# A transformer feed-forward reordered: up-projection bank by bank, half a down-projection per column tile, weight low parts on the vector engine

## What is computed

```python
def conv_gated_mlp(h, w_up, conv_w, conv_b, w_down):
    u = h @ w_up
    up = jnp.pad(u, ((0, 0), (1, 1), (0, 0)))
    u = up[:, :-2] * conv_w[0] + up[:, 1:-1] * conv_w[1] + up[:, 2:] * conv_w[2] + conv_b
    g, val = u[..., :D_FF], u[..., D_FF:]
    return (jax.nn.silu(g) * val) @ w_down
...
        x = x + jnp.concatenate([o_a, o_b, o_c], axis=-1) @ w_out[l]
        h = rmsnorm(x, norm_ffn[l])
        x = x + conv_gated_mlp(h, w_up[l], conv_w[l], conv_b[l], w_down[l])
```

## Time and profile before

| what | value |
|---|---|
| device time, median of 3 runs | 3556.5 us (3555.27 to 3556.6) |
| span of the profiled execution, first to last instruction | 3553.3 us |
| median time less that span | 3.2 us |
| mean granted TensorE clock | 0.943 of full speed |
| PE busy, share of the span | 88% |
| DVE / ACT / POOL busy | 61% / 39% / 31% |
| mean DMA traffic | 56 GB/s |

### The profile page before, as it was taken

How to read it: one execution, slowest core, us unless ns; L and a number is a source line. 1 busy time by engine, 2 the same in 40 slices (tenths; PEclk the granted TensorE clock), 3 DMA queues, 4 the chain that set the end, 5 groups by cost and what they waited for, 6 DMA issues and landing times.

```text
span 3553.3 us, 40957 instructions
## 1 busy us (share of the span) xinstructions
PE 3109.8 (88%) x13488; PEld 2397.5 (67%) x13488; DVE 2156.1 (61%) x2515; ACT 1396.9 (39%) x1917; POOL 1116.9 (31%) x532
## 2 busy tenths in 40 slices
PE   6888999667999999999799889986689999999996
PEld 5666777344777777777666667754467777777775
DVE  5864877997264445444567378779943545444545
ACT  3215888665321222111222188876633221111213
POOL 3113555552332112211221155455424112211222
PEclk8999999878999999999899999997889999999997
DMA  4332111111111111111033321111021111111112
GB/s 152 83 95 80 48 48 47 47 30 72 48 48 47 35 35 59 47 35 47 24 104 83 99 70 54 37 57 39 15 89 42 48 35 59 47 35 35 52 43 59
DMA packets 233542, 198.27 MB, mean 56 GB/s; under 512 B 49344, under 2 KB 207808, under 8 KB 233408
## 3 DMA queue, kind: packets, MB, share of 16 engines
q1 hardware_dynamic: 233408, 196.66, 18.2%
HBM read 163.07 MB, written 33.55 MB: 55 GB/s over the span
## 4 chain that ended last, share of the span: by engine, by line
PE 61%; DVE 17%; issue 14%; ACT 4%; DMA 2%; POOL 1%; DVEq 1%; ACTq 0%; SPq 0%; POOLq 0%
PE ps L1321 37%; PE ps L1533 10%; PE ps L1419 4%; PE ps L1450 4%; DVE ps L1137 2%; DVE ptl L1179 2%; PE ps L1430 2%; PE ps L1431 2%; DVE r L1080 1%; DVE xT L1249 1%; ACT prob L851 1%; DVE cv L1224 1%; PE ps L1462 1%; DVE rinv L1154 1%; ACT pth L881 1%
## 5 line engine op out<-in xcount | busy, mean ns | idle before, releaser
L1321 PE MATMUL ps<-xgh,w0h 128*128 128x512 f32 x1472 | 482.4, 409 | 65.3 <-DVE xT L1249 15.7
L1321 PE MATMUL ps<-xgh,w0l 128*128 128x512 f32 x1472 | 469.5, 400 | 0.0
L1321 PE MATMUL ps<-xgl,w0h 128*128 128x512 f32 x1472 | 468.6, 400 | 0.0
L1218 DVE TENSOR_TENSOR u<-ps,rstd 128x512 f32<-128x512 f32 x176 | 109.2, 683 | 581.3 <-PE ps L1321 581.0
L1450 PE MATMUL ps<-cst,prob 128*128 128x128 f32 x2048 | 334.9, 289 | 121.1 <-DVE prob L1155 58.0
L1450 PEld LDWEIGHTS ps<-cst,prob 128*128 128x128 f32 x2048 | 256.1, 147 | 270.1 <-DVE ptl L1179 140.9
L1419 PE MATMUL ps<-stack 128*128 128x512 f32 (+1 forms) x1152 | 349.0, 425 | 100.3 <-ACT prob L851 81.8
L1179 DVE TENSOR_TENSOR ptl<-ps,pth 128x512 fp32r<-128x512 f32 x512 | 348.7, 686 | 142.2 <-ACT pth L881 136.2
L851 ACT ACTIVATE prob<-ps,nmx 128x1024 f32<-128x1024 f32 x320 | 356.7, 1115 | 83.1 <-DVE nmx L1141 61.5
L955 ACT ACTIVATE cv<-u,vec 128x1024 f32<-128x1024 f32 x88 | 104.7, 1238 | 723.6 <-DVE u L1218 723.6
L1321 PEld LDWEIGHTS ps<-xgh,w0h 128*128 128x128 f32 x1472 | 279.8, 193 | 155.2 <-issue 28.0
(11 more groups left out here) (168 smaller groups left out, 5206.4 us busy)
## 6 DMA issues: line engine op xcount, KB each, us to landing
wraw<-in_w_up SPq DMA_DIRECT2D x88, 512.0 KB, 4.2
draw<-in_w_down SPq DMA_DIRECT2D x22, 1024.0 KB, 7.5
wraw<-in_w_in SPq DMA_DIRECT2D x36, 512.0 KB, 4.1
x_d<-xT SPq DMA_DIRECT2D x2, 4096.0 KB, 15.4
raw<-qa_d SPq DMA_DIRECT2D x32, 256.0 KB, 3.7
raw<-ka_d SPq DMA_DIRECT2D x32, 256.0 KB, 4.0
vraw<-v_d SPq DMA_DIRECT2D x32, 256.0 KB, 2.9
wraw<-in_w_out SPq DMA_DIRECT2D x16, 512.0 KB, 4.9
```

What stands on the lines that cost most here:

```text
L1218: ins = dve.tensor_tensor(u[:, c, 1 + b * HALF:1 + (b + 1) * HALF], ps[:, 4 * par + 2 * c + b, :], rstd[:, b * HALF:(b + 1) * HALF], ALU.mult)
L1321: ins = pe.matmul(outs[b], a, x_[:, b * HALF:(b + 1) * HALF], start=start and n == 0, stop=stop and n == 2)
```

## The change

The feed-forward is rewritten in steps of one column tile on every engine.

- PE: `up(f)` goes bank by bank: for each `c` and each token half `b` all 24 matmuls of that bank in a row, and `up_done` is raised after each bank. Tiles from 2 on always use banks 0 to 3; tile 1 uses 4 to 7. After each `up(f)` from `f` = 2 on comes one half (8 of 16 outputs) of the `down` of the group before, in banks 4 to 7. The first half's outputs too now wait for adds of four outputs before.
- DVE: `conv_in` is per `c`; the eight adds of the half `down` stand between `conv_in(f, 1)` and `outer_taps(f, 1)`. DVE also makes the low parts of the weights (`lo_up` of tiles 2 to 21, `lo_down` of groups 1 to 10); POOL keeps those of tiles 0 and 1 and group 0.
- ACT: `mid_tap` is per `c`, with the SiLU between the two; one `hi_up` in each step and one `hi_down` in each second step.
- `ah` and `al` have four slots for two; the loop runs four tiles long (`run_steps`: 4 tiles ahead of the loop, 4 passes of 4, 2 behind it). The program is built with `dynamic_dma_scratch_size=1024`, and SP's code is as it was.

```diff
-STEPS = {"pool layer": 24, "pool units": 2, "dve layer": 246, "dve units": 0, "dve group": 6}
+STEPS = {"pool layer": 24, "pool units": 2, "dve layer": 246, "dve units": 0, "dve quad": 12}
+QUAD = 4
+QUADS = 4
-        ah, al = sb(ph3, "ah", [P, 2, T], F32R), sb(ph3, "al", [P, 2, T], F32R)
+        ah, al = sb(ph3, "ah", [P, QUAD, T], F32R), sb(ph3, "al", [P, QUAD, T], F32R)
+        def run_steps(fn, eng, step=None):
+
+            for q in range(QUAD):
+                fn(0, q)
+            with eng.Fori(1, 1 + QUADS) as m:
...
+                for q in range(QUAD):
+                    fn(m, q)
...
+            for q in range(FT - QUAD * (1 + QUADS)):
+                fn(1 + QUADS, q)
```

POOL and ACT:

```diff
                 lo_up(1, 1)
                 lo_down(0)
-                lo_up(2, 0)
-                with pool.Fori(1, GROUPS - 1) as i:
-                    lo_up(i * 2 + 1, 1)
-                    lo_up(i * 2 + 2, 0)
-                    lo_down(i)
-                lo_up(FT - 1, 1)
-                lo_down(GROUPS - 1)
...
+                def act_step(m, q):
+
+                    f = m * QUAD + q
+                    mid_tap(f, 0)
+                    gate(f)
+                    mid_tap(f, 1)
+                    if not (isinstance(f, int) and f >= FT - 2):
+                        hi_up(f + 2, q % 2)
+                    hi_a(m, q)
+                    if q % 2 and not (isinstance(f, int) and f == 1):
+                        hi_down(m * 2 + q // 2)
```

DVE:

```diff
+                def lo_up(f, par):
+
+                    dve.wait_ge(up_hi, l * (KT + FT) + KT + f + 1)
+                    dve.tensor_tensor(up_weights(par)[1][:, :], wraw[:, :], up_weights(par)[0][:, :].bitcast(F32), ALU.subtract).then_inc(up_lo, 1)
...
+                def dve_ffn(m, q):
+
+                    f = m * QUAD + q
+                    first = isinstance(f, int)
+                    conv_in(f, 0)
                     outer_taps(f, 0)
+                    conv_in(f, 1)
+                    if not (first and f < 2):
+                        for j in range(8):
+                            add_down(m * 2 + (q // 2 - 1), 8 * (q % 2) + j)
                     outer_taps(f, 1)
+                    if not (first and f >= FT - 2):
+                        lo_up(f + 2, q % 2)
                     gate_value(f)
-                    lo_a(f, f)
...
+                    lo_a(f, q)
+                    if q % 2 and not (first and f == 1):
+                        lo_down(m * 2 + q // 2)
```

PE:

```diff
-                    for k in range(KT):
-                        if first and f == 0:
-                            pe.wait_ge(xg_lo, l * 16 + 8 + k + 1)
-                        for c in range(2):
-                            o = (2 * k + c) * P
-                            outs = [ps[:, 4 * par + 2 * c + b, :] for b in range(2)]
-                            ins = three(outs, up_weights(par)[0][:, o:o + P], up_weights(par)[1][:, o:o + P], xgh[:, k, :], xgl[:, k, :], k == 0, k == KT - 1)
-                    ins.then_inc(up_done, 1)
...
+                    base = 4 if first and f == 1 else 0
+                    for c in range(2):
+                        if not (first and f == 1):
+                            pe.wait_ge(u_ready, l * (2 * FT) + f * 2 - 1 + c)
+                        for b in range(2):
+                            for k in range(KT):
+                                o = (2 * k + c) * P
+                                for n, (a, x_) in enumerate(((wh, xgh), (wl, xgh), (wh, xgl))):
+                                    ins = pe.matmul(ps[:, base + 2 * c + b, :], a[:, o:o + P], x_[:, k, b * HALF:(b + 1) * HALF],
+                                                    start=k == 0 and n == 0, stop=k == KT - 1 and n == 2)
+                            ins.then_inc(up_done, 1)
...
-                        if j >= 4:
+                        if j >= 4 or not (isinstance(g, int) and g == 0):
                             pe.wait_ge(y_done, l * (16 * GROUPS) + g * 16 + j - 3)
...
+                def pe_step(m, q):
+
+                    f = m * QUAD + q
+                    up(f, q % 2)
...
+                    elif not (isinstance(f, int) and f == 1):
+                        pe.wait_ge(u_ready, l * (2 * FT) + f * 2)
+                        down(m * 2 + (q // 2 - 1), 2 - q // 2 * 2, 8 * (q % 2), 8 * (q % 2) + 8)
+
+                run_steps(pe_step, pe)
+                down(GROUPS - 1, (2 * GROUPS - 2) % QUAD, 0, 16)
```

More of the change, by code:

```diff
@@ L962, in gate, with hi_a @@
                     act.activation(cv[:, 0, :], cv[:, 0, :], ACT.Silu).then_inc(silu_done, 1)
[L964 to L974, removed]
-                gate(1)
-                hi_a(1, 1)
-                def act_group(i, last):
-                    mid_taps(i * 2)
-                    hi_up(i * 2 + 1, 1)
-                    gate(i * 2)
-                    if not last:
-                        hi_up(i * 2 + 2, 0)
-                    hi_a(i * 2, 0)
-                    hi_down(i)
-                    mid_taps(i * 2 + 1)
-                    gate(i * 2 + 1)
-                    hi_a(i * 2 + 1, 1)
-                with act.Fori(1, GROUPS - 1) as i:
-                    act_group(i, False)
-                act_group(GROUPS - 1, True)
-                act.wait_ge(up_done, l * FT + FT)
+                def hi_a(m, q):
+                    act.wait_ge(prod_done, l * FT + m * QUAD + q + 1)
+                    if not (isinstance(m, int) and m == 0):
+                        act.wait_ge(down_done, l * (16 * GROUPS) + m * 32 + (q // 2 * 16 - 16))
+                    act.activation(ah[:, q, :], cv[:, 0, :], ACT.Copy).then_inc(a_hi, 1)
+                def act_step(m, q):
[8 more added lines that the diff above has]
+                        hi_down(m * 2 + q // 2)
+                run_steps(act_step, act)
+                act.wait_ge(up_done, l * (4 * FT) + 4 * FT)
                 for n in range(2):
@@ L1523, in down @@
-                def down(g):
+                        for k in range(KT):
+                            pe.wait_ge(xg_lo, l * 16 + 8 + k + 1)
+                            for c in range(2):
+                                o = (2 * k + c) * P
+                                for n, (a, x_) in enumerate(((wh, xgh), (wl, xgh), (wh, xgl))):
+                                    for b in range(2):
+                                        ins = pe.matmul(ps[:, 2 * c + b, :], a[:, o:o + P], x_[:, k, b * HALF:(b + 1) * HALF],
+                                                        start=k == 0 and n == 0, stop=k == KT - 1 and n == 2)
+                                        if k == KT - 1 and n == 2:
+                                            ins.then_inc(up_done, 1)
@@ new lines, in up @@
+                        return
+                    if first and f == 1:
+                        pe.wait_ge(root_done, l + 1)
+                    base = 4 if first and f == 1 else 0
+                    for c in range(2):
+                        if not (first and f == 1):
+                            pe.wait_ge(u_ready, l * (2 * FT) + f * 2 - 1 + c)
+                        for b in range(2):
+                            for k in range(KT):
+                                o = (2 * k + c) * P
+                                for n, (a, x_) in enumerate(((wh, xgh), (wl, xgh), (wh, xgl))):
+                                    ins = pe.matmul(ps[:, base + 2 * c + b, :], a[:, o:o + P], x_[:, k, b * HALF:(b + 1) * HALF],
+                                                    start=k == 0 and n == 0, stop=k == KT - 1 and n == 2)
+                            ins.then_inc(up_done, 1)
```

96 lines of the change are left out of this document (33 added, 63 removed).

## The result

| | before | after |
|---|---|---|
| device time, median | 3555.9 us (3549.2 to 3556.6, 4 runs) | 3433.1 us (3429.9 to 3436.3, 4 runs) |
| span of the profiled execution | 3553.3 us | 3428.0 us |
| mean granted clock | 0.943 | 0.954 |

The ratio is 0.9653, 95% interval 0.9636 to 0.9671. The forecast was 3411 us with a range of 3402 to 3444. The time is inside the range, but it is that of rival 1 (3435 us), not of the likeliest case.

What follows compares the result with a forecast made beforehand. PE was taken to set the pace, with 117.5 us of surplus in the feed-forwards. Terms 117.5 + 14.0 - 10.0 + 23.8 = 145.3 us off 3553.3 give 3408.0; the median's 3.2 more makes 3411 us, range 3402 to 3444.

Steps and rivals of the forecast that it cites:

- rival 1: In `up`: the pace stays at 0.2324 us a matmul, 23.8 us of gain are missing, 3435 us; chance 0.34.
- the likeliest case: Whole kernel: all four terms hold, `up` taking `down`'s pace, 145.3 us gained, 3411 us; chance 0.46.
- stalls inside the groups: Feed-forward loop: PE runs through without waiting for DVE, regaining all 117.5 us of surplus in two layers.
- end of a layer: Ahead of the last `down`: PE's wait falls from 14.23 to 7.2 us, 14.0 gained in all.
- start of a layer: At `up(2)`: a new 3.4 us wait for `u_ready`, 5.0 a layer with slow matmuls, 10.0 lost in all.
- pace of `up`: In `up`: matmul spacing falls from 0.2324 to `down`'s 0.2265 us, 23.8 us gained over 4032 matmuls.
- Rival 3: On DVE: taps take 5.37 us without POOL too, PE waits 5.3 us a step, 3689 us; chance 0.04.
- I take the row that the new form is nearest to: In `up`: `down`-like form, new weights each matmul and 24 in a row per bank, was taken to give 0.2265 us.
- Rival 2: In the steps: PE's clock drops, 1.65 us in each of 40, 3477 us; chance 0.12 with other small waits.
- Rival 4: In the longer loop: instructions arrive late at branches, eating the gain, 3556 us; chance 0.04 with anything leaving time unchanged.
- The low end of the range: At the start of a layer: no wait of PE at `up(2)`, given as 3402 us.

Runs made afterwards that it cites:

- e1: Changed kernel with the low parts of the weights made on POOL again (also written e1_pool_lows); 3446.8 us, ratio 0.9701.
- e3: Kernel before with only the weights' low parts moved to DVE, from tile 3 and group 1 on, taps still between the adds; 3466.9 us, ratio 0.9763.
- e2b_pairs_half: Changed kernel with `up` in halves by `c`, matmul pairs sharing a weight block and alternating between two banks; 3432.1 us, ratio 0.9662.
- p1_incs: Changed kernel with one more semaphore increment at every sixth matmul of `up`, which nothing waits on; 3433.1 us, ratio 0.9648.
- p4_down_weights_up: Changed kernel with `down` of groups 0 to 9 taking its weights from `up`'s buffers, so its output is not the feed-forward's; 3434.4 us, one run.
- p3_down_reads_x: Changed kernel with `down` of groups 0 to 9 reading `xgh`, `xgl` as moving operand, so its output is not the feed-forward's; 3442.7 us, one run.
- p5_align: Changed kernel with the constants allocated ahead of `xgh` and `xgl`, which then start at multiples of 1024 bytes; 3410.3 us, ratio 0.9578.
- p6_shift_ah: Changed kernel with 128 bytes of padding ahead of `ah` and `al`, so they start 128 past a multiple of 1024; 3441.0 us, ratio 0.9667.
- i1_ends: Changed kernel with `up(2)` waiting only for tile 0 and the last `down`'s weights split ahead of `hi_a` and `lo_a`; 3426.7 us, ratio 0.9632.
- b2_before_align: Kernel before with the constants allocated ahead of `xgh` and `xgl`, which then start at multiples of 1024 bytes; 3517.4 us, ratio 0.9882.

## Why the prediction was right, and where it was wrong

By its own terms, per layer, from the start of `up(1)` to the start of the last `down`:

| term | predicted, us | measured, us |
|---|---|---|
| stalls inside the groups | -58.7 | -58.7: nothing of the surplus is left, PE busy 643.28 of 643.28 |
| end of a layer | -7.0 | -4.2: 10.06 for 14.23 |
| start of a layer | +5.0 | +1.9: 1017.06 - 992.75 = 24.31 for 1017.08 - 994.67 = 22.41 |
| pace of `up` | -11.9 | +1.8: 0.2333 for 0.2324, 2016 matmuls |
| sum | -72.6 | -59.2 worked out; -59.1 and -59.3 measured |

- **Stalls: right.** DVE was in time in every step, and the tap, the subtraction and the add cost what the rows before had shown. Rival 3 falls: the taps are short once POOL's subtraction isn't beside them (e1, e3). But the change has two remedies for one stall, and with only one of them most of it is gone.
- **Pace of `up`: wrong, and as large as the whole miss.** It is 13.7 us a layer, 27 in all, and the time came out 22 above the forecast. The step that failed is "I take the row that the new form is nearest to". Form had nothing to do with it: e2b_pairs_half has the old form and the new form's pace, p1_incs and p4_down_weights_up leave it, p3_down_reads_x, p5_align and p6_shift_ah move it by the moving operand alone. Rival 1 had the right reason, operands and buffers that don't change, with 0.34. The argument against it, that the paces are steady within each form, was true just as much for "within each operand", and the rows couldn't tell the two apart. The 0.2333 for 0.2324 is a second, smaller thing: p6_shift_ah has 0.2324 in the same order, and p3_down_reads_x has 0.2333 in its first layer and 0.2324 in its second, so it isn't the order either; what makes it stays open.
- **End of a layer: right in kind, 2.8 us short.** The sum followed only the path through `al`. It missed that `hi_down` and `lo_down` of group 10 are queued behind `hi_a` and `lo_a`, though both are in the diff. i1_ends took 2.0 us of it back.
- **Start of a layer: wait there, over-priced by 3.1 us.** `up(2)` came 1.9 us later (1.65 of idle time) and not 3.4. Of the 1.5 between, 1.3 is the SiLU's table load, which ACT made at 1002.01 us (`1002.01 1.28 ACT L970 ACT_TABLE_LOAD`), while the taps were still running on DVE, instead of in the serial path. The 1.65 us for slow matmuls didn't come: none followed this wait. They did in p5_align, and in one layer of two in e1_pool_lows; what decides it is open, and the rows of before couldn't price it.
- **Rival 2 didn't come**: granted clock 1.00 over 643 us, with a bank handed over every 5.6 us. The Trainium skill's warning on bank cycling (TensorE: Matmul & The Clock Gate, A second HAM failure mode: psum-queue depth-cycling) isn't borne out by this row. **Rival 4 didn't come** either: the steps are all 33.28 us, those with a branch among them.
- **What was luck.** The time lies in the range because the range took in rival 1; with the likeliest case alone it is missed by 22 us. The errors at the two ends, 2.8 and 3.1 us a layer, cancel, and 6.8 us came off outside that stretch, which no term foresaw. The low end of the range is a slip of 1 us: with no wait at the start the sum gives 3411.2 - 10.0 = 3401 and not 3402.

## What to carry to other kernels

When two streams of matmuls of one shape keep different paces at one clock, compare what they read and where it lies before crediting the order they are written in. Where an engine is stretched by another, look for which pairs of instructions lie beside each other: moving one of them in time can be worth as much as moving it to another engine. At the ends of a loop follow every semaphore that the last consumer waits for, the weights' too, not only the one that was last before.

## What the runs showed of the hardware

- The spacing of 128x512 matmuls was 0.2265 to 0.2270 us with the moving operand's tensors starting at a multiple of 1024 bytes in each partition, and 0.2324 to 0.2333 with them 128 bytes past one, in four placements of `xgh` and `xgl` (before, after, p5_align, b2_before_align) and three of `ah` and `al` (before, after, p6_shift_ah). Only these two offsets were tried; that 1024 is the step that matters, rather than 256 or 512, is not shown. The matmuls of L1416 lie 0.231 us apart in the mean (of spacings of 0.20 to 0.24 us) though their `stack` tiles start at multiples of 1024 in the changed kernel, so this isn't the only thing that sets a spacing.
- A wait of PE of 1.65 us was followed by matmuls at a granted clock of 1.00, one of 2.23 us, at the same place of nearly the same program, by about 4 us at 0.57. One of 3.72 us (e1_pool_lows) was followed by 1.00 in one layer and by 4 us at 0.64 in the other, so a longer wait doesn't by itself bring the slow matmuls.
- POOL's subtraction stretched a tap with two SBUF tensors from 1.3 to 5.4 us and in e1_pool_lows left adds with one PSUM and one SBUF source at 0.69 us.
